# A fused two-block transformer kernel: eight modulation slots become four, and thirty-two VectorE pieces in place of sixteen

## The reference, cut to what matters

```python
mod   = silu(c)     @ w_mod + b_mod      # 1024 -> 6 x 1024, for the latent rows
mod_c = silu(c_ctx) @ w_mod + b_mod      # the same for the context rows
sh_a, sc_a, g_a, sh_f, sc_f, g_f = split(mod, 6)
csh_a, csc_a, ... = split(mod_c, 6)      # only these two are used
h  = rmsnorm(x, norm_attn) * (1 + sc_a) + sh_a
hc = rmsnorm(ctx, norm_attn) * (1 + csc_a) + csh_a
x  = x + g_a * token_mixers(h, hc, ...)
h2 = rmsnorm(x, norm_ffn) * (1 + sc_f) + sh_f
x  = x + g_f * moe(h2)
```

## Time and profile before

| | |
|---|---|
| runs | 634.45, 634.45, 637.77 us |
| median | 634.45 us |
| profiled execution, span from the first to the last instruction | 632.1 us |
| PE, PE weight loads, DVE, ACT, POOL busy | 90%, 59%, 47%, 34%, 6% |
| bytes read from HBM | 191.21 MB, 304 GB/s over the span |
| mean granted clock of TensorE | 0.976 |

### The profile page before, as it was taken

How to read it: one execution, slowest core, us unless ns; L and a number is a source line. 1 busy time by engine, 2 the same in 40 slices (tenths; PEclk the granted TensorE clock), 3 DMA queues, 4 the chain that set the end, 5 groups by cost and what they waited for, 6 DMA issues and landing times.

```text
span 632.1 us, 8828 instructions
## 1 busy us (share of the span) xinstructions
PE 568.5 (90%) x3510; PEld 372.4 (59%) x3510; DVE 298.7 (47%) x701; ACT 213.9 (34%) x453; POOL 38.9 (6%) x68
## 2 busy tenths in 40 slices
PE   8999999999999999999998999999989765675685
PEld 7988977777867887868774444455443411321232
DVE  2556467675668977774747766234220100100002
ACT  3345443654523622665337754131110100100002
POOL 2000000000000000010004433000000000000000
PEclk9999999999999999999999999999999997897899
DMA  9984965659679887435658333768999999999994
GB/s 358 331 284 166 378 272 199 255 227 383 268 311 432 321 302 290 173 113 234 245 242 336 163 101 134 311 244 324 399 430 427 425 428 426 428 423 431 426 419 175
DMA packets 23069, 193.36 MB, mean 306 GB/s; under 512 B 4211, under 2 KB 5619, under 8 KB 11253
## 3 DMA queue, kind: packets, MB, share of 16 engines
q1 hardware_dynamic: 21732, 190.11, 75.4%
q0 software_dynamic: 288, 1.57, 0.6%
q10 hardware_dynamic: 1008, 1.12, 0.6%
HBM read 191.21 MB, written 1.06 MB: 304 GB/s over the span
## 4 chain that ended last, share of the span: by engine, by line
PE 65%; DMA 20%; DVE 6%; ACT 3%; SPq 2%; issue 1%; POOL 1%; ACTq 0%; POOLq 0%; DVEq 0%
PE bank L1240 27%; DMA ring<-in_stream 19%; PE bank L1904 6%; PE bank L1217 5%; PE bank L1228 5%; PE bank L1840 2%; PE bank L1286 2%; PE bank L1768 2%; PE bank L1703 2%; PE bank L1555 2%; PE bank L1826 2%; SPq L833 2%; PE bank L1616 1%; PE bank L1950 1%; PE bank L1662 1%
## 5 line engine op out<-in xcount | busy, mean ns | idle before, releaser
L1240 PE MATMUL bank<-weight_parts,u_parts 128*128 128x512 f32 (+1 forms) x384 | 116.5, 386 | 0.8 <-DVE weight_parts L2216 0.4
L1240 PEld LDWEIGHTS bank<-weight_parts,u_parts 128*128 128x128 f32 x384 | 69.9, 188 | 17.0 <-issue 2.7
L2216 DVE TENSOR_TENSOR weight_parts<-ring,weight_parts 128x1024 fp32r<-128x1024 f32 x56 | 66.5, 1222 | 23.9 <-ACT weight_parts L859 21.9
L859 ACT ACTIVATE weight_parts<-ring 128x1024 fp32r<-128x1024 f32 x56 | 57.2, 1055 | 14.5 <-PE bank L1240 14.1
L1240 PE MATMUL bank<-weight_parts,x_parts 128*128 128x512 f32 (+1 forms) x128 | 48.4, 378 | 0.0
L1240 PE MATMUL bank<-u_parts,weight_parts 128*128 128x256 f32 x192 | 36.5, 286 | 0.9 <-DVE weight_parts L2216 0.7
L1193 POOL TENSOR_TENSOR small<-small 128x1 f32<-128x1 f32 (+1 forms) x14 | 8.5, 608 | 417.8 <-DVE small L2649 200.0
L921 ACT ACTIVATE sp<-sp,small 128x128 f32<-128x128 f32 (+1 forms) x48 | 21.3, 444 | 32.0 <-DVE small L2125 32.0
L1240 PEld LDWEIGHTS bank<-u_parts,weight_parts 128*128 128x128 f32 x192 | 30.4, 191 | 2.4 <-issue 1.2
L1141 ACT ACTIVATE sp<-bank 128x512 f32<-128x512 f32 x4 | 2.4, 597 | 74.1 <-PE bank L1904 74.1
L2621 DVE SCALAR_TENSOR_TENSOR sp<-sp,bank 128x512 f32<-128x512 f32 x4 | 2.7, 685 | 52.2 <-ACT sp L1141 52.2
(11 more groups left out here) (367 smaller groups left out, 1064.1 us busy)
## 6 DMA issues: line engine op xcount, KB each, us to landing
ring<-in_stream SPq DMA_DIRECT2D x35, 2048.0 KB, 9.7
qk<-in_stream SPq DMA_DIRECT2D x9, 2048.0 KB, 12.5
parts<-in_stream SPq DMA_DIRECT2D x9, 2048.0 KB, 20.0
tabs<-in_stream SPq DMA_DIRECT2D x6, 2048.0 KB, 17.1
mo<-in_stream SPq DMA_DIRECT2D x5, 2048.0 KB, 26.9
vvc<-in_stream SPq DMA_DIRECT2D x5, 2048.0 KB, 30.0
ring<-in_stream SPq DMA_DIRECT2D x6, 1024.0 KB, 6.4
vvc<-in_vecs SPq DMA_DIRECT2D x12, 512.0 KB, 8.6
```

The lines of the kernel that those rows point to most:

```text
L859: ins = act.activation(dst, src, ACT.Copy, scale=scale)
L1240: ins = pe_.matmul(o, lhs(a, c, i), rhs(b, c, i), start=(c == 0 and n == 0), stop=(c == chunks - 1 and n == 2))
L2216: dve.tensor_tensor(quarter(low, name, q), quarter(slot(name), name, q), quarter(high, name, q).bitcast(F32), ALU.subtract).then_inc(split ...
```

## The change

Slots M4 to M7 leave the stream. Columns g_a and sh_f become sixteen more pieces on DVE, 32 in all. The first eight pieces hold g_a in an order in which the gate row can be written to HBM straight from the column tile. Eleven pieces (EARLY_VECS) run between kb1 and cO1 and are loaded, at M0 to W8, into four rooms in mo, lat and zz that are empty then; the others use the rooms of before. ACT gets waits so that it writes those rooms only after the pieces. The spreading of the condition moves from SP to POOL, behind a memset at the start of its loop. The second half of the kept modulation, its bias, its wait and the transposes modT1 are gone. With fewer slots W9 to C1 sit in other buffers (W9 in 1, W10 in 4, W11 in 1, WB in 0, C0 in 4, WO0 in 1, C1 in 4).

```diff
-STREAM = (["W0", "W1", "W2", "W3", "W4", "M0", "WC", "W5", "M1", "W6", "M2", "W7", "M3", "W8", "M4", "W9", "M5",
-           "WA", "M6", "W10", "M7", "W11", "WB", "C0", "WO0", "C1", "WO1", "X2", "KU0",
+STREAM = (["W0", "W1", "W2", "W3", "W4", "M0", "WC", "W5", "M1", "W6", "M2", "W7", "M3", "W8", "W9",
+           "WA", "W10", "W11", "WB", "C0", "WO0", "C1", "WO1", "X2", "KU0",
            "X1", "X0", "QU", "KU1", "OUT0", "OUT1"]
...
-LATE = {"C0": 0, "WO0": 4, "C1": 1, "WO1": 0, "KU0": 1, "X2": 4, "X1": 1, "X0": 0, "QU": 1, "KU1": 0, "OUT0": 2, "OUT1": 3}
+LATE = {"C0": 4, "WO0": 1, "C1": 4, "WO1": 0, "KU0": 1, "X2": 4, "X1": 1, "X0": 0, "QU": 1, "KU1": 0, "OUT0": 2, "OUT1": 3}
...
-         "hT00", "hT01", "ckv01", "ckv11", "modT1", "hT10", "hT11",
+         "hT00", "hT01", "ckv01", "ckv11", "hT10", "hT11",
...
-MOD_AFTER = {"qb1": 0, "cT": 1, "za0": 2, "za1": 3, "cO1": 4, "gA11": 5, "wa10": 6, "wa11": 7}
-KEPT_AFTER = {"za1": 0, "wa11": 1}
-N_VEC = 16
-VEC_AFTER = {"wa10": [0], "ybT1": [1], "cxT11": [2, 3, 4, 5], "wb00": [6, 7], "mT00": [8, 9], "wo00": [10, 11, 12, 13], "cc0": [14, 15]}
-VEC_LOADS = {"W9": [0, 1], "M7": [2, 3], "W11": [4, 5], "WO0": [6, 7, 8, 9], "C1": [10, 11], "WO1": [12, 13, 14, 15]}
+MOD_AFTER = {"qb1": 0, "cT": 1, "za0": 2, "za1": 3}
+N_VEC = 32
+GATE_VECS = 8
+EARLY_VECS = 11
+VEC_AFTER = {"kb1": [0, 1], "vb0": [2], "vb1": [3], "za0": [4, 5], "za1": [6, 7], "zb0": [8], "zb1": [9], "cO1": [10],
+             "wa00": [11], "wa10": [12], "wa11": [13], "gB00": [14], "cxT11": [15, 16, 17], "gB01": [18], "wb00": [19, 20],
+             "mT00": [21], "wo00": [22, 23, 24], "cc0": [25, 26], "wo01": [27], "ckv10": [28], "hT01": [29], "ckv11": [30],
+             "xa02": [31]}
+VEC_LOADS = {"M0": [0, 1, 2, 3], "M2": [4, 5], "W7": [6, 7], "M3": [8, 9], "W8": [10], "W10": [12, 13, 11, 14],
+             "W11": [15, 16], "WB": [17], "C0": [18, 19, 20, 21], "WO0": [22, 23, 24], "WO1": [25, 26, 27, 28],
+             "X2": [29, 30], "KU0": [31]}
...
+        vec_rooms = [[view(mo, 0, 1024), view(mo, 1024, 1024), view(lat, 0, 1024), view(zz, 1024, 1024)],
+                     [view(vc, 3072, 1024), view(vc, 4096, 1024), view(vv, 0, 1024), view(pt, 0, 1024)]]
+        vec_at = [vec_rooms[k >= EARLY_VECS][k % 4] for k in range(N_VEC)]
...
-                    for i in range(2):
-                        eng.dma_start(bias[i], A["mod_bias"][:, 512 * i:512 * i + 512]).then_inc(bias_in[i], 16)
-                if name == "W5":
-                    eng.wait_ge(cond_ready, 1)
-                    eng.dma_start(cond_row.rearrange("o (p c) -> p (o c)", p=P), csil_col).then_inc(cond_row_out, 16)
-                if name == "M1":
-                    eng.wait_ge(cond_row_out, 16)
-                    eng.dma_start(csil_row, cond_row.to_broadcast([P, D])).then_inc(cond_row_in, 16)
...
+                    eng.dma_start(bias, A["mod_bias"]).then_inc(bias_in, 16)
+                if name == "W9":
+                    eng.wait_ge(vec_biased, 1)
+                    eng.dma_start(gate_row.rearrange("o (p c) -> p (o c)", p=P), mc[:, 0, 16:16 + GATE_VECS])\
+                       .then_inc(gate_row_out, 16)
+                if name == "X1":
+                    eng.wait_ge(gate_row_out, 16)
+                    eng.wait_ge(vec_used, 29)
                     eng.dma_start(gG, gate_row.to_broadcast([P, D])).then_inc(gate_row_in, 16)
...
                 for k in VEC_LOADS.get(name, []):
-                    if k == 2:
+                    if k == 0:
+                        eng.wait_ge(u_split, 2)
+                    if k in (11, 14):
                         eng.wait_ge(pvs, len(UNITS))
                     if k >= 4:
                         eng.wait_ge(vec_used, k - 3)
...
+                        if name == "zb0":
+                            eng.wait_ge(vec_used, 8)
...
+                        if name == "gA00":
+                            eng.wait_ge(vec_used, 10)
...
+                        if name == "yaT0":
+                            eng.wait_ge(vec_used, EARLY_VECS)
...
+            def spread_condition():
+                eng.wait_ge(cond_ready, 1)
+                eng.dma_start(cond_row.rearrange("o (p c) -> p (o c)", p=P), csil_col).then_inc(cond_row_out, 16)
+                eng.wait_ge(cond_row_out, 16)
+                eng.dma_start(csil_row, cond_row.to_broadcast([P, D])).then_inc(cond_row_in, 16)
...
                     eng.wait_ge(blocks_ready, 2)
                     pool.memset(view(vc, 512, 512), 0.0).then_inc(zeroed, 1)
+                    spread_condition()
...
                 if k % 8 == 7:
                     a = k - 7
                     eng.wait_ge(vec_used, k + 1)
-                    own(dve.tensor_tensor(mc[:, 0, 32 + a:40 + a], mc[:, 0, 32 + a:40 + a], vec_bias[:, a:a + 8], ALU.add))
-                    if k == 7:
+                    dve.tensor_tensor(mc[:, 0, 16 + a:24 + a], mc[:, 0, 16 + a:24 + a], vec_bias[:, a:a + 8], ALU.add)\
+                       .then_inc(vec_biased, 1)
+                    if k == 23:
+                        eng.wait_ge(vec_biased, 3)
                         own(dve.scalar_tensor_tensor(scl[:, 2, :], mc[:, 0, 32:40], 1.0, nff, ALU.add, ALU.mult))
```

More of the change, by code:

```diff
@@ L176, in schedule @@
             out.append(("mod", MOD_AFTER[name]))
-        if name in KEPT_AFTER:
-            out.append(("mod kept", KEPT_AFTER[name]))
+        if name == "za1":
+            out.append(("mod kept", 0))
         for k in VEC_AFTER.get(name, []):
@@ L501, in build @@
         wmask_in = sem("wmask_in")
-        bias_in = [sem(f"bias_in{i}") for i in range(2)]
+        bias_in = sem("bias_in")
+        vec_biased = sem("vec_biased")
         out_done = sem("out_done")
@@ L789, in _ @@
                     eng.dma_start(tabs[:, 0:8 * CAUSAL], A["nsa_table"]).then_inc(nsa_table_in, 16)
-                    for i in range(2):
-                        eng.dma_start(bias[i], A["mod_bias"][:, 512 * i:512 * i + 512]).then_inc(bias_in[i], 16)
-                if name == "W5":
-                    eng.wait_ge(cond_ready, 1)
-                    eng.dma_start(cond_row.rearrange("o (p c) -> p (o c)", p=P), csil_col).then_inc(cond_row_out, 16)
-                if name == "M1":
-                    eng.wait_ge(cond_row_out, 16)
-                    eng.dma_start(csil_row, cond_row.to_broadcast([P, D])).then_inc(cond_row_in, 16)
-                if name == "WO0":
-                    eng.wait_ge(mod_kept, 2)
-                    for h in range(2):
-                        eng.dma_start(gate_row[:, 512 * h:512 * h + 512], mod[32 * h:32 * h + 1, :]).then_inc(gate_row_out, 16)
-                if name == "KU0":
-                    eng.wait_ge(gate_row_out, 32)
-                    eng.wait_ge(vec_used, 13)
+                    eng.dma_start(bias, A["mod_bias"]).then_inc(bias_in, 16)
[6 more added lines that the diff above has]
+                    eng.wait_ge(vec_used, 29)
                     eng.dma_start(gG, gate_row.to_broadcast([P, D])).then_inc(gate_row_in, 16)
@@ L1035, in _ @@
                         if name == "xa01":
-                            kept(eng, "modT1")
-                            eng.wait_ge(gate_row_out, 32)
+                            kept(eng, "modT0")
                             eng.wait_ge(vec_used, N_VEC)
@@ L1304, in shift_sums @@
             def shift_sums(name):
-                kept(eng, "modT1")
+                eng.wait_ge(vec_biased, 2)
                 eng.wait_ge(const_in, 16 * (len(constants) + 1))
@@ L2233, in _ @@
                 elif kind == "mod kept":
-                    eng.wait_ge(mod_used, 4 * n + 4)
-                    eng.wait_ge(bias_in[n], 16)
-                    dve.tensor_tensor(mod, MB[:, :], bias[n], ALU.add).then_inc(mod_kept, 1)
+                    eng.wait_ge(mod_used, 4)
+                    eng.wait_ge(bias_in, 16)
+                    dve.tensor_tensor(mod, MB[:, :], bias, ALU.add).then_inc(mod_kept, 1)
                 elif kind == "vec":
@@ L2752, in stream_of @@
     wm = chunks(a["w_mod_2"][0])
-    for n in range(8):
+    for n in range(4):
         flat[f"M{n}"] = wm[:, 2 * (n % 4):2 * (n % 4) + 2, 2048 * (n // 4):2048 * (n // 4) + 2048].reshape(P, -1)
@@ L2774, in host_arrays @@
     cond = np.stack([col(a["c_2"]), col(a["c_ctx_2"])], 2).reshape(P, -1)
-    mod_bias = np.zeros((4, 32, 3, 512), np.float32)
-    mod_bias[:, 0:2] = a["b_mod_2"][0].reshape(3, 4, 1, 512).transpose(1, 2, 0, 3)
+    mod_bias = np.zeros((4, 32, 512), np.float32)
+    mod_bias[:, 0:2] = a["b_mod_2"][0, 0:2048].reshape(4, 1, 512)
+    late = np.arange(2048, 6 * D)
+    late[0:D] = 2048 + np.arange(D).reshape(P, GATE_VECS).T.reshape(-1)
     return {
```

19 lines of the change are left out of this document (8 added, 11 removed).

## The result

The changed kernel takes 639.32 us (median of 13 runs, 636.90 to 641.05) against 634.45 (632.31 to 637.77, 13 runs): ratio 1.0068, 95% interval 1.0052 to 1.0084. It is **slower by 0.7%**, some 4.3 us by the ratio (the two medians lie 4.9 apart), where 633.9 had been forecast with a range to 638.0. The profiled run of the changed kernel is its fastest, 636.9 us with a span of 634.7; 2.6 us more span than before.

The account below looks back on a forecast made before the run. Matmuls set the pace to about 440 us, then loads do. The terms 1.65 - 3 x 1.85 + 2.3 + 0.95 = -0.65, say -0.6, took 634.45 to 633.9 us; range 630.8 to 638.0.

Parts of the forecast that it names:

- DVE's pile: Ten early pieces on DVE before gA00: most fall into waits, gA00 begins 1.65 us late (bounds 0 and 11.5).
- M5, M6, M7 gone: After gA00, dropping three slots on the path gains 1.85 us each; TensorE stands at -3.85 us from 190 to 265.
- pieces 27 and 28: Behind the block-1 norms, two pieces in DVE's order on the path: +2.3 us, so xa02 begins at -1.55.
- xa02 to xa01: Block-1 norms' tail: TensorE waits about 0.9 us before xa12 for the last hl_parts row; +0.95 in the sum.
- sum at the hand-over: All terms up to the first product behind the xa stretch that waits for a split again: -0.65 us.
- The clock: Slower rival: the pause of 4.4 us before gA00 lowers TensorE's clock; taken at 2.8 us, 636.6 us, chance 0.12.
- The fuller case (over 5 us): Slower rival before gA00: more than 5 of the early pieces' 11.5 us stay; at 5.5, 637.7 us, chance 0.08.
- 29 and 30: Two pieces between hT01 and hT10: 2.3 us on DVE, less 0.3; TensorE waits about 0.9 us before xa12.
- M1 and the spread of the condition: Moving the spread to GpSimd's queue costs nothing, with 9 us of cover; M1 may start 0.84 us earlier.
- vec 11's load in time: Loaded from 177.3, piece 11 ends near 183.5 and ybT0's low part near 184.1, just as TensorE wants that bank.
- X2 not late: X2's load lands at 257.1 with 0.8 us to spare; slower rival: 4.1 us late, 638.0 us, chance 0.12.

Follow-up runs that it names:

- all ten thin: The changed kernel with pieces 0 to 9 multiplied over 8 of their 1024 columns, loads whole: 634.32 us, ratio 1.0012.
- the kernel with the loads behind W8: The changed kernel with the loads of pieces 8 and 9 issued behind W8 and no longer right behind M3: 638.56 us, ratio 1.0078.
- the thin slots, alone and with the pause: The kernel before with M4 to M7's products over 8 columns: 631.41 us; with two unread DVE multiplications ahead of cO0's addition as well: 634.21 us.

## Why the prediction was wrong

Each term is a difference against the kernel before, from the first profile of the changed kernel; the pieces' share at gA00 is counted from M3's start.

| step of the forecast | forecast | measured |
|---|---|---|
| gA00 begins later, pieces 8 and 9 (DVE's pile) | +1.65 | +1.97 |
| gA00 begins later, M3 late by its load | 0 | +0.97 |
| gA00's product | 0 | +1.59 |
| M5, M6, M7 gone | -5.55 | -4.83 |
| pieces 27 and 28 | +2.3 | +1.98 |
| xa02 to xa01 | +0.95 | +1.56 (0.92 with the clock up) |
| sum at the hand-over | -0.65 | +3.24 |

**The clock** is the step that failed. It was a rival with a chance of 0.12, at the one new pause I had looked at, and argued away by "no pause of this profile, the longest some 1.2 us, moved the clock". That row could not say anything of a pause three times as long. I had the pause right, 4.4 us forecast and 3.71 measured, and two rows of a fall behind a wait of 2.97; calling the expert stage a special case was the mistake. The second pause I didn't see at all: the two pieces ahead of xa02 that I had priced at 2.3 us together also make TensorE stand for 3.59 where it had stood for 1.21, and 0.6 of the difference is the place that modT1's transposes had filled. The falls cost 1.59 us at gA00 and 0.64 in the xa stretch, 2.2 of the 3.9 us between forecast and profile, and filling the pauses returned 2.0 of the time. The rest of the 3.9 is M3's load (0.97), M5 to M7 (0.72) and pieces 8 and 9 (0.32), less 0.32 at 27 and 28. The rival as I had priced it, 636.6 us, stands close to the profiled run's 636.9, but by luck: these other terms and its own size were wrong. The Trainium skill (TensorE: Matmul & The Clock Gate, section "Why this matters for your kernels") asks for no long pause between bursts of matmuls, and by that rule the slow case was the likeliest. The traces now agree with it in the dense stage too, for pauses of 3.6 us and more; behind four of 2.03 to 2.12 us the clock fell as well.

**gA00's start** was late by 2.94 us in place of 1.65, and DVE's pile was the smaller part of the error. Pieces 8 and 9 cost 2.0 us from M3 to gA00, where the walk had let part of them fall into waits; pieces 0 to 7 cost nothing (26.12 us from M3 to gA00 with all ten thin). The other 0.97 is M3, which waited 1.00 us for its load, a term I had not in the sum. That wait was 0.17 to 0.92 us in nine other profiles with whole early loads and 1.83 in a tenth; without such loads it did not occur. The fuller case (over 5 us) did not come.

**M5 to M7** gave 0.7 us less than 1.85 each (-4.83, read just ahead of the block-1 norms). With the later start and the slow product in front, TensorE was 0.5 us ahead at 205, where the forecast had 3.85. The chain of the changed kernel, where PE had M5 before:

```profile
173.20 5.50 PE bank L1254 x24
...
178.73 1.06 ACT weight_parts L860
...
179.81 1.23 DVE weight_parts L2230
...
181.17 0.87 DVE mo L2158 x4
...
183.77 0.70 DVE tabs L2405
```

The slots had covered the end of WA's split and the read-out of a bank, which now stand in the chain: DVE's reciprocal comes after the last quarter of the split, at 181.04, and the product at 188.31 waits 0.34 us for the read-out. Of the 0.7, about 0.3 is lost by 184.51, 0.2 by 188.31, and the last 0.2 between 207 and 221 us, for a cause that I did not look for. The forecast let the slots go at full price "if the next data are there", and did not check what they had covered.

**Pieces 27 and 28** were right within 0.3 us. **29 and 30** were right in mechanism but hidden: once the clock stays up, xa12 waits 0.57 us for the rows and the stretch takes 0.92 us more than before, against the 0.95 forecast; while xa02 is slow, xa12 does not wait at all.

**Right:** M1 and the spread of the condition, worth nothing (on GpSimd's queue its two transfers took 5.5 us each, so cover was ample); vec 11's load in time; X2 not late (the split shows no wait for a load, and SP issued it at 253.10); the slots' removal worth less than it seemed, since the order of DVE gives it back.

**Open:** the median of the changed kernel lies 2.4 us above its two profiles, which agree with each other. The clock's price differs from run to run (7.3 to 8.6 us for the same product behind the same 3.71 us), which can account for some 1.3 of it at the first pause, and for another 0.8 at the second, where hT10's transposes varied too (an estimate from the kernel with the loads behind W8, whose profiled run took 639.32). No profile of a run of the changed kernel near its median shows it. For the thin slots, alone and with the pause, the median lies 1.8 us off the profiled run too.

## What to carry to other kernels

Work taken off TensorE is worth only what its successors' data allow, and the hole it leaves may cost more than the work: ask of each new pause how long it is, and price the matmuls behind it at the lower clock too when it exceeds the longest that the profile shows as harmless. Before a helper engine takes over work, write down its idle stretches and put the pieces there; here the same four pieces cost 3.5 us in the norms' tail, and nothing with two of them 25 us earlier and two behind xa02. Read a late start from the step ahead of it too: a third of gA00's delay was M3's load. Where a pause must stay, a few unread transposes of its length bought back 1.6 us at no cost.

## What was unexpected of the hardware

The lower clock behind a pause is short but not of one length: gA00's 24 matmuls lost 1.6 us in seven profiles and 2.4 to 2.9 in four. A pause of 2.03 us caused it and one of 2.25, behind sixteen full-width matmuls, did not. And a program with less work on TensorE came out slower, about half of it for this (2.2 us by the profile, of 4.3).
